# Latent attention's scores: unrotated part of two heads on row halves, rotated part on row quarters

## The reference, cut to what matters

```python
q = (rms_norm(cq, g_q_a) @ w_q_up).reshape(B, S, MLA_HEADS, MLA_NOPE + MLA_ROPE)   # 8 heads of 64 + 32
q_nope, q_pe = q[..., :MLA_NOPE], q[..., MLA_NOPE:]
kv = (rms_norm(ckv, g_kv_a) @ w_kv_up).reshape(B, S, MLA_HEADS, MLA_NOPE + MLA_V)
k_nope, v_m = kv[..., :MLA_NOPE], kv[..., MLA_NOPE:]
q_pe = apply_rope(q_pe, ang[:, :, None, :])
k_pe = apply_rope(kpe, ang)[:, :, None, :]
qm = jnp.concatenate([q_nope, q_pe], axis=-1)
km = jnp.concatenate([k_nope, jnp.broadcast_to(k_pe, (B, S, MLA_HEADS, MLA_ROPE))], axis=-1)
o_mla = causal_block_attention(qm, km, v_m)     # scores qm @ km.T, causal mask, softmax, times v_m
```

## Time and profile before

| | |
|---|---|
| median of three runs | 2457.43 us (2453.64 to 2457.77) |
| the profiled execution | 2458.28 us, its span 2456.9 us |
| PE busy | 2346.2 us (95% of the span) |
| DVE busy | 1249.6 us (51%) |
| ACT busy | 582.8 us (24%) |
| queries stage | about 79 to 119 us of the span |
| attention stage of latent attention | about 128 to 340 us of the span |
| its score matmuls | 96-row forms, 192 records; mask 64 records |

### The profile page before, as it was taken

The page is one execution under the profiler, slowest core; times in us unless marked ns, Lnnn a source line. Parts: engine busy times, 40 slices in busy tenths (PEclk is TensorE's granted clock), DMA queues, the critical chain, the costliest instruction groups (busy, mean ns, idle before and its releaser), DMA issues.

```text
span 2456.9 us, 25964 instructions
## 1 busy us (share of the span) xinstructions
PE 2346.2 (95%) x9779; PEld 1370.9 (56%) x9779; DVE 1249.6 (51%) x2584; ACT 582.8 (24%) x1345; POOL 636.3 (26%) x528
## 2 busy tenths in 40 slices
PE   8999999999999999999999999999999999699993
PEld 5676657764444444444444677744464644488772
DVE  5444425444567777877753466665501336511124
ACT  3344423321122221222211111111100221011113
POOL 1000000044543454453272000007341045112213
PEclk9999999999999999999999999999999999799997
DMA  5000210122110110110235201003250213658987
GB/s 171 1 1 1 86 35 1 47 68 86 35 35 18 35 35 18 35 35 20 93 87 157 70 13 44 34 1 139 101 199 7 69 46 141 211 148 263 274 248 215
DMA packets 145211, 203.88 MB, mean 83 GB/s; under 512 B 16820, under 2 KB 101684, under 8 KB 145080
## 3 DMA queue, kind: packets, MB, share of 16 engines
q1 hardware_dynamic: 138168, 176.99, 21.9%
q0 software_dynamic: 6912, 25.17, 4.3%
HBM read 164.37 MB, written 37.77 MB: 82 GB/s over the span
## 4 chain that ended last, share of the span: by engine, by line
PE 85%; POOL 3%; DVE 3%; DMA 2%; issue 2%; ACT 1%; POOLq 0%; DVEq 0%; ACTq 0%
PE banks L171 79%; PE banks L174 6%; DMA arena<-x_scratch,slots 1%; POOL arena L1430 1%; POOL arena L1448 1%; DVE arena L3806 0%; DVE arena L3813 0%; DVE arena L896 0%; POOL arena L1425 0%; POOL arena L1431 0%; DMA x_scratch<-arena,places 0%; POOL arena L1433 0%; POOL x_scratch L3519 0%; POOL arena L1459 0%; ACT arena L3138 0%
## 5 line engine op out<-in xcount | busy, mean ns | idle before, releaser
L171 PE MATMUL banks<-arena 128*128 128x512 f32 (+16 forms) x8131 | 2183.9, 456 | 30.2 <-DVE arena L3374 5.7
L171 PEld LDWEIGHTS banks<-arena 128*128 128x128 f32 (+6 forms) x8131 | 1197.3, 183 | 920.6 <-issue 831.3
L174 PE MATMUL banks<-arena 128*128 128x128 f32 (+2 forms) x1552 | 222.2, 280 | 41.5 <-DVE arena L448 10.4
L174 PEld LDWEIGHTS banks<-arena 128*128 128x128 f32 (+2 forms) x1552 | 178.6, 142 | 113.8 <-issue 66.1
L2161 POOL TENSOR_TENSOR arena<-arena 128x512 f32<-128x512 f32 (+3 forms) x160 | 154.5, 967 | 166.4 <-ACT arena L1972 146.7
L259 POOL TENSOR_TENSOR arena<-arena 128x1 f32<-128x1 f32 (+1 forms) x88 | 65.0, 741 | 486.0 <-DVE arena L2697 312.0
L1425 POOL TENSOR_TENSOR arena<-arena 128x512 f32<-128x512 f32 x4 | 9.3, 2321 | 572.7 <-PE banks L174 453.2
L1972 ACT ACTIVATE arena<-arena 128x512 f32<-128x512 f32 (+4 forms) x160 | 81.6, 576 | 315.7 <-DVE arena L2063 314.5
L2031 DVE TENSOR_TENSOR arena<-arena 128x512 f32<-128x512 f32 (+3 forms) x160 | 106.4, 723 | 28.3 <-ACT arena L1964 28.3
L3519 POOL DMA_INDIRECT x_scratch<-arena,places x24 | 37.8, 1577 | 204.4 <-DVE arena L3672 204.4
L2063 DVE TENSOR_TENSOR arena<-arena,banks 128x512 f32<-128x512 f32 (+4 forms) x160 | 89.5, 624 | 1.1 <-PE banks L174 1.1
(11 more groups left out here) (346 smaller groups left out, 1735.0 us busy)
## 6 DMA issues: line engine op xcount, KB each, us to landing
x_scratch<-arena SPq DMA_DIRECT2D x40, 512.0 KB, 2.9
arena<-in_o_w_in_dram SPq DMA_DIRECT2D x32, 512.0 KB, 5.4
arena<-x_scratch SPq DMA_DIRECT2D x32, 512.0 KB, 5.4
arena<-in_w_gate_dram SPq DMA_DIRECT2D x16, 1024.0 KB, 14.8
arena<-in_w_up_dram SPq DMA_DIRECT2D x16, 1024.0 KB, 17.3
arena<-in_w_down_dram SPq DMA_DIRECT2D x16, 1024.0 KB, 19.8
arena<-in_x_dram SPq DMA_DIRECT2D x16, 512.0 KB, 5.0
arena<-in_w_in_dram SPq DMA_DIRECT2D x16, 512.0 KB, 7.0
```

The costliest lines, as they stand in the source:

```text
L171: return pe.matmul(o, a, b, start=start, stop=stop)
L174: return pe.transpose(o, a, ident)
```

## The change

- The projected queries are copied in two parts: the unrotated 64 values of 8 heads into the first half of `QTOK` (heads in order), the rotated 32 values into a buffer of their own, `QPE`. Each group of four heads takes two ACT instructions (256 and 128 elements) in place of one of 384.
- DVE rotates in `QPE`, and the last addition is done twice: it writes the rotated values of each pair of heads two times into the second half of `QTOK`, so that a block of 128 values there is (head 0, head 1, head 0, head 1).
- The eight transposes of a tile are then of 128 x 128 (`turn_tile`): for each pair one of both heads' unrotated values and one of the four rotated parts.
- The keys of a pair stand in one buffer: rows 0 to 63 head 0, rows 64 to 127 head 1. ACT copies a unit with one instruction of 128 rows. The rotated keys stand four times in `KPE4`, one copy for each row quarter.
- The scores of a step: for each block of up to 512 keys one matmul on rows 0 to 63 (head 0) and one on rows 64 to 127 (head 1); then for each block and head a matmul on 32 rows that adds the rotated part (the first 512 keys on quarters 0 and 1, the keys behind them on quarters 2 and 3); then the two masks. Both heads now wait for the exponentials of both heads of the step before, and both `s_done` signals come from the two masks at the end.

```diff
+        QPE = [scr(56 + i, 256) for i in range(2)]
+        QPT = [scr(58 + i, 256) for i in range(2)]
+        QN8 = QT8.rearrange("p (a b) s -> p b a s", b=2)
+        KPE4 = KA[2]
...
-                    for half in range(2):
-                        tb = bank(4 + half)
-                        for j in range(4):
-                            h = 4 * half + j
-                            m = tr(tb[0:96, 128 * j:128 * j + 128], QTOK[t % 2][:, 96 * h:96 * h + 96])
-                        m.then_inc(q_turned.sem, 1)
+                    turn_tile(QTOK[t % 2], q_turned)
...
-                        act.activation(qt[:, 384 * n:384 * n + 384], sb[:, 512 * n:512 * n + 384], ACT.Copy, scale=MSC)
+                        heads = tiled(sb[:, 512 * n:512 * n + 384], 4)
+                        act.activation(tiled(qt[:, 256 * n:256 * n + 256], 4), heads[:, :, 0:64], ACT.Copy, scale=MSC)
+                        act.activation(tiled(QPE[i % 2][:, 128 * n:128 * n + 128], 4), heads[:, :, 64:96], ACT.Copy, scale=MSC)
...
-                    act.activation(QT8[0:96, 0:4, 128 * t:128 * t + 128], tiled(bank(4)[0:96, :], 4),
-                                   ACT.Copy).then_inc(qt_a.sem, 1)
+                    act.activation(QN8[:, 0, :, 128 * t:128 * t + 128], tiled(bank(4), 4), ACT.Copy).then_inc(qt_a.sem, 1)
...
-                    q3 = tiled(QTOK[i % 2][:, 0:768], 8)[:, :, 64:96]
-                    tmp = tiled(QTOK[i % 2][:, 768:1024], 8)
+                    q3, tmp = tiled(QPE[i % 2], 8), tiled(QPT[i % 2], 8)
...
-                    vec.tensor_tensor(q3, q3, tmp, ADD).then_inc(q_roped.sem, 1)
+                    twice = QTOK[i % 2][:, 512:1024].rearrange("p (a c d) -> p c a d", a=4, c=2)
+                    for c in range(2):
+                        m = vec.tensor_tensor(twice[:, c], tiled(QPE[i % 2], 4), tiled(QPT[i % 2], 4), ADD)
+                    m.then_inc(q_roped.sem, 1)
                 if 1 <= i <= 4:
-                    vec.tensor_copy(KA[i - 1][64:96, :], KPT).then_inc(kpe_done.sem, 1)
+                    vec.tensor_copy(KPE4[32 * i - 32:32 * i, :], KPT).then_inc(kpe_done.sem, 1)
...
-                    vec.tensor_copy(QT8[0:96, 4:8, 128 * t:128 * t + 128],
-                                    tiled(bank(5)[0:96, :], 4)).then_inc(qt_v.sem, 1)
+                    vec.tensor_copy(QN8[:, 1, :, 128 * t:128 * t + 128], tiled(bank(5), 4)).then_inc(qt_v.sem, 1)
...
-                for h in range(2):
-                    m = act.activation(KA[2 * (q % 2) + h][0:64, 512 * n:512 * n + 512], zb[64 * h:64 * h + 64, :], ACT.Copy)
-                m.then_inc(f_a.sem, 1)
+                act.activation(KA[q % 2][:, 512 * n:512 * n + 512], zb, ACT.Copy).then_inc(f_a.sem, 1)
...
             P.wait_ge(f_a, mla.fa + 10 * p + 5)
+            P.wait_ge(ex_done, mla.ex + 2 * s)
+            sc = [bank(2 * h, 2) for h in range(2)]
+            q = 128 * t
+            for b in range(0, n, 512):
+                w = min(512, n - b)
+                for h in range(2):
+                    rows = slice(64 * h, 64 * h + 64)
+                    mm(sc[h][:, b:b + w], QT8[rows, 2 * p, q:q + 128], KA[p % 2][rows, b:b + w], True, False)
+            for b in range(0, n, 512):
+                w = min(512, n - b)
+                for h in range(2):
+                    r = 32 * (2 * (b > 0) + h)
+                    mm(sc[h][:, b:b + w], QT8[r:r + 32, 2 * p + 1, q:q + 128], KPE4[r:r + 32, b:b + w], False, b + w != n)
             for h in range(2):
-                P.wait_ge(ex_done, mla.ex + 2 * s - 1 + h)
-                sc = bank(2 * h, 2)
-                for b in range(0, n, 512):
-                    w = min(512, n - b)
-                    mm(sc[:, b:b + w], QT8[0:96, 2 * p + h, 128 * t:128 * t + 128], KA[2 * (p % 2) + h][0:96, b:b + w], True,
-                       b + w != n)
-                mm(sc[:, n - 128:n], identb[:, :], maskq[:, :], False, True).then_inc(s_done.sem, 1)
+                mm(sc[h][:, n - 128:n], identb[:, :], maskq[:, :], False, True).then_inc(s_done.sem, 1)
```

## The result

The median after the change is **2474.53 us** (four runs, 2471.03 to 2476.26), that of before in the same comparison 2457.60 us (four runs, 2453.64 to 2458.02): 16.9 us more, a ratio of 1.0072 with the interval 1.006 to 1.0084. The change makes the kernel slower. The prediction was 2473.6 us, 16.2 us more.

A forecast was written before the change was run, and what follows sets the result against it. PE was taken to set the end in both changed stages, with its waits for L708 on top. 7.4 (PE) + 7.6 (late chain) + 1.2 (queries) = +16.2 us, forecast 2473.6 us, range 2464 to 2484.

The forecast's parts named there:

- Part 1: Score matmuls on PE: four quarters at once save 8.6 us at t = 4 to 7, masks at the end 1.6.
- about half a microsecond: Sign of being wrong: scores at t = 0 to 3 not longer by about this much.
- Part 2: Array form switches in each scores step: full to halves 0.20, halves to quarters 0.20, quarters to full 0.15; 17.6 us lost.
- the third: Switch from quarters to full array for the 16-bit mask: 0.15 us taken, bounds 0.09 and 0.20.
- PE's balance: PE's own work in the attention stage: 17.6 - 8.6 - 1.6 = +7.4 us.
- hidden switches: Rival: weights of one form load while another runs, so switches cost 0; 2456 us, no change; chance 0.04.
- Part 3: Softmax chain at t = 6 and 7 starts later, so PE waits longer for L708; 7.6 us lost.
- In other steps ... I cost them at nothing: Attention steps other than t = 6 and 7: shorter maxima and exponentials or longer cover, so no loss from late signals.
- the cover: PE's other work while the softmax chain runs; if it fails, some tenths lost in each t = 4.
- Part 4: Queries stage: an added DVE addition and split ACT copies lengthen its chain; 1.2 us lost, bounds 0.5 and 2.
- The clock: Rival: clock falls after 1.8 us waits at t = 7, up to 1.7 us each; four give 2480; chance 0.10.
- the prediction's own signs of being wrong: Scores at t = 0 to 3 not longer, L708's waits unchanged, or PE clock falls in the attention stage.

## Why the prediction was right

- **What bounds it.** PE's own instructions and the wait for L708 were the two accounts, and they hold 5.3 + 7.17 = 12.47 of the 16.67 us found.
- **Part 1, columns: right.** Four quarters run at once; taking two of them away costs 8.6 us, as computed. The Trainium skill's factor of 3.07 in place of four (page "TensorE: Matmul & The Clock Gate", section "Measured speedup vs the span model") is for four matmuls at once against one after the other, which no run here compares. From two quarters to four no loss of that kind shows: eight passes on four last 1.14 us and four on two 1.13. The steps t = 0 to 3 gained nothing and became 0.35 us longer, plus 0.09 of drain ahead, as "about half a microsecond" said. The masks side by side gained 0.06 a step rather than 0.05.
- **Part 2, switches: right for the first two, too high for the third.** Halves to quarters costs 0.20 us (0.97 against 0.77 at t = 0). That a finer split of rows is a change of form that drains the engine is what the Trainium skill says (page "TensorEngine Tiling (Array Packing)", section "Key Properties"), and this trace agrees. The switch to the 16-bit mask is 0.10, not 0.15: the drain alone. That is 1.6 us of the 2.1 by which PE's balance (5.3) stayed under the 7.4 predicted; the masks are another 0.3. The point from which the rival "hidden switches" decides, 0.066 us a switch, was far off.
- **Part 3, late chain: right in place and size.** 7.17 us against 7.6, and the late signals alone bring the same 10.1 us of waits. The step that failed is "In other steps ... I cost them at nothing": t = 4 lost 0.28 us in each pair, 1.1 in all. The prediction had priced that at some tenths if the cover failed, and it failed, in the place that it named. PE's eight transposes at t = 4 in before, then in after, and last the emptying on DVE, late behind the maxima, for which PE stops after four of them:

```profile
148.08 1.04 PE L174 MATMUL banks<-arena 128*128 128x128 f32 x8
...
151.49 1.32 PE L174 MATMUL banks<-arena 128*128 128x128 f32 x8
...
151.35 0.69 DVE L743 COPY arena<-banks 128x512 f32<-128x512 f32 x1
```

- **Part 4, queries: right**, 1.5 against 1.2, and in the chain that it named: the starts of the tiles' transposes give 0.3 in the first tile and 1.0 in the later ones, where 0.2 and 1.0 were computed; 0.2 come behind the last tile, 0.09 of them the drain before the first scores, which the 5.3 hold too. One reading of the rows is wrong there, without harm to the sum: 82.85 is not a tile's projection but the start of the transposes of the tile before, so 4.59 and 4.33 are distances between transposes.
- **The clock** counted as a rival, with the wait of 1.8 us at t = 7 as its ground (1.56 of idle time was measured, 1.72 with the end of the record ahead of it). One fall came in the profiled execution, 1.6 us, where the rival priced four; but a fall in the stage was also one of the prediction's own signs of being wrong, and the forecast had put the clock at nothing. After with the early emptying has no such wait and no fall in the stage; the kernel with the late signals alone has the wait and a clock of 1.00 throughout. And after itself has the wait in all four pairs, with a fall behind the first alone. So the wait doesn't decide it by itself. Over all traces it is a condition, as far as they go: the six kernels that have the waits at t = 6 and 7 of 1.3 to 1.6 us show five falls behind their 24 waits at t = 7, each within 2 us of one, and the five kernels without these waits show none in the stage.
- The sum came out within 1 us in part by errors that cancel: PE 2.1 too high and the wait 0.43, against 1.1 of t = 4, 1.6 of the clock and 0.3 of the queries. The mechanism and the sign of each term that was costed were right; that the total came out so close was luck.

## What to carry to other kernels

Splitting the rows of the array pays only where the columns that it saves in one step outlast its switches: here 0.5 us a step for three switches, against savings of 0 to 0.86 us in a step, and only t = 6 and 7 came out ahead. When matmuls of two heads are put side by side, their signals come together and late; look what stands behind the consumers (here maximum, exponential and the emptying of a bank), because that loss was larger than PE's own. And where an engine waits for a long chain, see whether it can first do the short copy that another engine waits for: one reordering on ACT took 10 us of waits from after and brought the kernel before to 2452 us.

## What the runs showed of the hardware that was not expected

- A switch of row form has two prices: 0.10 us into a 16-bit mask on the whole array, 0.20 us into 32-bit passes on other rows (0.09 to 0.10 before the first pass, 0.10 for the weights of the second: in the weight loads at t = 7 above they come only as the new form starts).
- Two more quarters beside two busy ones cost 0.01 us in 1.13.
- The same wait of 1.56 us of PE was followed by 3.4 us at a granted clock of 0.50 in one pair of after and by none in the kernel with the late signals (5 of 24 such waits in six kernels), and falls come at different places in kernels that differ by a few copies (177.4 us in after, 231.2 and 350.7 with the copies moved). In these comparisons the medians of the kernels with the copies moved and with halves alone didn't show parts of 1 to 2 us that the rows' starts do.
